# The weight stream's linears read both halves of x as one operand of 512 columns, and ScalarE makes the high half of the weights

## The chip, the core and the metric

The kernel is one program on one core of one Trainium2 chip. The metric is the time of one execution on the device, in microseconds; the median of three runs is the number that counts. The engines are TensorE (PE in the profile, with PEld for its weight loads), VectorE (DVE), ScalarE (ACT), GpSimd (POOL) and SyncE (SP, which here issues the loads of weights).

## What is computed

A two-layer block of 256 tokens with 1024 features (two SwiGLU networks, a mixer of convolution, HGRN2 and RWKV7, and cross-attention over 256 memory rows), and after it a second two-layer block (attention and a mixture of 64 experts). The change touches the plain matrix products of the first block and one of the second:

```python
def swiglu_ffn(x, w_in, w_out):
    gate, up = jnp.split(x @ w_in, 2, axis=-1)
    return (jax.nn.silu(gate) * up) @ w_out

for l in range(DEPTH):                                              # DEPTH = 2
    h = h + FFN_RES * swiglu_ffn(rmsnorm(h, ffn1_norm[l]), ffn1_w_in[l], ffn1_w_out[l])
    p = rmsnorm(h, mix_norm[l]) @ w_mix_in[l]
    ...
    h = h + y @ w_mix_out[l]
    h = h + memory_cross_attention(rmsnorm(h, xattn_norm[l]), rmsnorm(mem, mem_norm[l]),
                                   xattn_wq[l], xattn_wkv[l], xattn_wo[l])
    h = h + FFN_RES * swiglu_ffn(rmsnorm(h, ffn2_norm[l]), ffn2_w_in[l], ffn2_w_out[l])
```

The results are float32. w_in is 1024 x 5632, w_out 2816 x 1024, w_mix_in 1024 x 3712.

## The kernel before

**Split products.** TensorE gets its operands in the type float32r, which keeps fewer bits. A float32 number is therefore split in two: its rounded "high" half, and the rest ("low"). A product a·b is computed as ah·bh + ah·bl + al·bh. `mm3` (L370) issues these three matmuls for one block of weights: the 128 x 128 block is the stationary operand (its high half twice, its low half once) and the moving operand is one half of x^T, 128 features by 256 tokens. All three add up in the same 256 columns of a PSUM bank.

**The stream.** `Stream` (from L109) feeds the weights in the order in which they are used. A chunk is 32 blocks (128 x 4096 numbers, 2 MB). SyncE loads chunk c into one of three slots when TensorE has finished chunk c-3. `split(c)` makes the halves: one operation casts the raw weights into one of two high slots (L130), the second subtracts and writes the low half over the raw weights (L131). When TensorE's program comes to the first block of chunk c, `blocks` marks chunk c-1 as released and records `split(c+1)` at this place. The cast of c+1 waits until its data has arrived and until TensorE has finished chunk c-1, since that chunk held the high slot. `cancel(c)` turns the split of a chunk that is used unsplit into small idle operations; `prepare` records a split ahead of its place.

**Queues.** Each engine's work is a list in program order (`Queue`, L33). Operations of VectorE and ScalarE also wait for the one before them. So a waiting operation holds all that stands behind it on its engine, and the order of recording is the order of execution.

**The linears.** `linear` (L425) computes nm tiles of 128 output features; each takes one of eight PSUM banks and sums over kt blocks, and `evac` then takes the result out of the bank. `ffn` has its own loop for w_in: for each of FT = 22 tiles i it computes gate and up (eight blocks each) in the two halves of one bank, multiplies both by the inverse RMS in one operation of 512 columns, applies SiLU to the gate on ScalarE (`silu[i]`), and `product(i-1)` multiplies gate and up and splits the result (the cast on VectorE, the subtraction on GpSimd). w_in is 352 blocks, 11 chunks; w_out is 176 blocks, eight tiles of 22. In w_out, w_mix_out (64 blocks) and xattn_wo (64) the evacuation adds to the residual X, and `Normed.add` makes both halves of the next stage's input and a Square on ScalarE. Ahead of w_mix_out, `memory_squares` lets ScalarE square eight tiles of the memory, which wait for their load. Ahead of the first linear stand eight scalings and eight squares of x on ScalarE.

The linears of 256 tokens are, for each of the two layers, 2 x 528 blocks of the two feed-forward networks, 232 of w_mix_in, 64 each of w_mix_out, xattn_wq, the K half of xattn_wkv and xattn_wo; with na_w_out (64) that is 3152 blocks, 98.5 chunks. The V half of xattn_wkv and the second block's other products use the stream as well but other forms of matmul; the experts have their own buffers and their own splitting.

## Time and profile before

| | before |
|---|---|
| median of 3 runs | 3906.31 us |
| runs | 3905.23 to 3908.49 us |
| the profiled execution's own time | 3905.64 us |
| its span, first to last instruction | 3903.5 us |
| TensorE busy | 3486.5 us (89%) |
| VectorE busy | 2813.5 us (72%) |
| ScalarE busy | 1163.5 us (30%) |
| mean granted TensorE clock | 0.94 |

A share of busy time is a mean over stages: the first block of the computation lasts until about 1770 us, the experts fill 2105 to 2790 and 3190 to 3840 us. What a change is worth is read in the stage in which it acts, from the wait that ends last there. TensorE's granted clock is given as a share of 2.4 GHz.

### The profile page before, as it was taken

The numbers are of one execution on the slowest core, as the hardware profiler recorded it, in microseconds if no ns is written. First come the engines' busy times: TensorE is split into PE (matmuls) and PEld (weight loads), VectorE is DVE, ScalarE is ACT, GpSimd is POOL, SyncE is SP. The second block draws the span as 40 slices with busy tenths as digits, with TensorE's granted clock in tenths as the row PEclk, the third lists the DMA queues.
The fourth block names the chain that finished last, engine by engine and source line by source line (L and its number), as shares of the span: only waits on it lengthen the run. The fifth ranks groups of instructions, "written<-read, shape, count | busy, mean of one in ns | idle before, by whom it ended". The sixth has DMA issues, their size and how long they took to land. (4 is left out here: it accounts for less than half of the span.)

```text
span 3903.5 us, 51678 instructions
## 1 busy us (share of the span) xinstructions
PE 3486.5 (89%) x20728; PEld 2837.5 (73%) x20728; DVE 2813.5 (72%) x3240; ACT 1163.5 (30%) x1539; POOL 439.6 (11%) x459
## 2 busy tenths in 40 slices
PE   8996878999996879997888999999559889999995
PEld 8993778999993778996555776677348656776774
DVE  8866687888876677887757777777274677777774
ACT  1003101101003101101322565565210245655562
POOL 0000200000000200100001121122001111221220
PEclk9997889999996889998999999999779989999998
DMA  6547023454556023551015999999433159999993
GB/s 238 185 183 280 1 86 124 172 191 175 192 196 256 1 78 128 184 195 65 22 53 195 363 368 363 359 359 372 180 137 119 54 191 336 338 346 335 337 340 127
DMA packets 118927, 802.65 MB, mean 206 GB/s; under 512 B 33808, under 2 KB 34832, under 8 KB 48272
## 3 DMA queue, kind: packets, MB, share of 16 engines
q1 hardware_dynamic: 77040, 714.17, 49.6%
q0 software_dynamic: 40592, 83.99, 6.0%
q8 instruction: 166, 2.72, 0.3%
q10 hardware_dynamic: 1040, 1.05, 0.1%
q14 instruction: 89, 0.73, 0.1%
HBM read 812.18 MB, written 71.83 MB: 226 GB/s over the span
## 5 line engine op out<-in xcount | busy, mean ns | idle before, releaser
L368 PE MATMUL ps<-arena_r,ring_r 128*128 128x256 f32 (+1 forms) x10224 | 1305.1, 289 | 84.2 <-DVE arena L400 24.7
L368 PEld LDWEIGHTS ps<-arena_r,ring_r 128*128 128x128 f32 x10224 | 1265.3, 190 | 120.9 <-DVE arena L400 25.8
L1875 PE MATMUL ps<-ring_r,arena_r 128*128 128x512 f32 x1880 | 555.1, 398 | 7.0 <-DVE arena_r L1891 7.0
L416 ACT ACTIVATE arena<-arena 128x256 f32<-128x256 f32 (+3 forms) x298 | 144.4, 485 | 1292.0 <-DVE arena L400 782.8
L131 DVE TENSOR_TENSOR ring_r<-ring,ring_r 128x4096 fp32r<-128x4096 f32 (+2 forms) x117 | 509.7, 4356 | 4.0
L1875 PE MATMUL ps<-ring,arena 128*128 128x512 f32 x1032 | 464.1, 592 | 1.6 <-DVE arena L1927 1.6
L1872 DVE TENSOR_TENSOR ring_r<-ring,arena_hi 128x2048 fp32r<-128x2048 f32 x152 | 348.5, 2293 | 97.0 <-ACT arena_hi L1871 89.1
L1875 PEld LDWEIGHTS ps<-ring_r,arena_r 128*128 128x128 f32 x1880 | 351.9, 189 | 82.3 <-DVE arena_r L1891 7.9
L1875 PE MATMUL ps<-arena_hi,arena_r 128*128 128x512 f32 x1216 | 400.8, 397 | 0.0
L368 PE MATMUL ps<-arena 128*128 128x128 f32 (+5 forms) x1728 | 262.7, 338 | 105.1 <-DMA arena<-yd_dram 40.5
L130 DVE CAST ring_r<-ring 128x4096 fp32r<-128x4096 f32 (+2 forms) x117 | 291.9, 2495 | 71.3 <-PE ps L368 59.0
L1875 PEld LDWEIGHTS ps<-ring,arena 128*128 128x128 f32 x1032 | 195.4, 190 | 198.0 <-issue 185.2
L368 PEld LDWEIGHTS ps<-arena 128*128 128x128 f32 (+1 forms) x1728 | 205.7, 216 | 155.8 <-ACT arena L420 52.1
L1872 DVE TENSOR_TENSOR ring_r<-ring,ring_r 128x2048 fp32r<-128x2048 f32 x106 | 243.0, 2292 | 74.8 <-ACT ring_r L1871 69.0
L1871 ACT CAST arena_hi<-ring 128x2048 fp32r<-128x2048 f32 x152 | 290.0, 1908 | 13.7 <-ACT arena_r L1890 0.7
L1875 PEld LDWEIGHTS ps<-arena_hi,arena_r 128*128 128x128 f32 x1216 | 229.1, 188 | 48.7
L1891 DVE TENSOR_TENSOR arena_r<-ps,arena_r 128x512 fp32r<-128x512 f32 x258 | 178.4, 692 | 97.6 <-ACT arena_r L1890 83.7
L1956 POOL DMA_INDIRECT yd_dram<-arena,small x129 | 129.8, 1006 | 1015.1 <-ACT arena_r L1890 930.3
L1871 ACT CAST ring_r<-ring 128x2048 fp32r<-128x2048 f32 x106 | 202.6, 1912 | 36.8 <-PE ps L368 19.7
L400 POOL TENSOR_TENSOR arena_r<-arena,arena_r 128x256 fp32r<-128x256 f32 (+1 forms) x104 | 84.2, 810 | 978.5 <-DVE arena_r L388 978.5
L1941 ACT COPY arena<-ps 128x512 f32<-128x512 f32 x129 | 75.5, 585 | 397.2 <-PE ps L1875 397.2
L421 DVE COPY arena<-ps 128x128 f32<-128x128 f32 (+3 forms) x172 | 68.8, 400 | 152.2 <-PE ps L368 139.3
(192 smaller groups left out, 3333.4 us busy)
## 6 DMA issues: line engine op xcount, KB each, us to landing
ring<-wexp_dram SPq DMA_DIRECT2D x387, 1024.0 KB, 8.3
ring<-stream_dram SPq DMA_DIRECT2D x145, 2048.0 KB, 7.7
arena<-yd_dram POOLq DMA_DIRECT2D x12, 2048.0 KB, 10.2
xd_dram<-arena POOLq DMA_DIRECT2D x6, 512.0 KB, 9.9
consts_sb<-consts_dram SPq DMA_DIRECT2D x1, 2241.5 KB, 15.8
arena<-xd_dram,small POOLq DMA_INDIRECT x129, 10.3
yd_dram<-arena,small POOLq DMA_INDIRECT x129, 8.2
arena<-mem_dram POOLq DMA_DIRECT2D x2, 1024.0 KB, 5.3
```

The lines of the kernel that those rows point to most:

```text
L130: self.dve(lambda e, h=h, r=r: e.tensor_copy(h, r), self.arrived(c), self.released.get(c - NHI), after)
L131: toks.append(self.dve(lambda e, h=h, r=r, w=w: e.tensor_tensor(w, r, h.bitcast(F32), ALU.subtract)))
L368: return PE(lambda e: e.matmul(ps, lhsT=lhsT, rhs=rhs, start=start, stop=stop, skip_group_check=True), *after, inc=inc)
L400: return q(lambda e: e.tensor_tensor(out_, a, b, op), *after, **kw)
L416: return ACTQ(lambda e: e.activation(out_, a, f, bias=bias, scale=scale), *after, **kw)
L421: return q(lambda e: e.tensor_copy(out_, a), *after, **kw)
L1871: t = Ac(lambda e: e.copy(hi, src), got(n), free)
L1872: split_tok[n] = Dv(lambda e: e.tensor_tensor(lo, src, hi.bitcast(F32), ALU.subtract), t)
L1875: return P(lambda e: e.matmul(out_, lhsT=x, rhs=y, start=st_, stop=sp_, skip_group_check=True), *after, inc=inc)
L1891: t2 = Dv(lambda e, hi=hi, lo=lo, ps=ps: e.tensor_tensor(lo, ps[:, :], hi.bitcast(F32), ALU.subtract), t2)
L1941: fn = (lambda e, dst=dst, ps=ps: e.copy(dst, ps[0:S, :])) if nn else \
L1956: Po.raw(lambda e: e.indirect_dma_start(out=yd, out_offset=bass.IndirectOffsetOnAxis(ap=pair_of[0:S, b0 + i:b0 + i + 1], axis=0), in_=YB[i ...
```

## The change

`mm3` is replaced in the 256-token linears by `mm2`: one matmul of the weights' high half with 512 columns, the low and the high half of x side by side (an access pattern of two pieces, `pair`), and one of the weights' low half with the 256 columns of x's high half. The first writes all 512 columns of a bank, the second adds to the upper 256. The two halves of the bank are then added: ScalarE copies the lower one to a temporary, VectorE adds the upper one. In w_in, gate and up take a bank each, and the multiplication by the inverse RMS then works on SBUF. In `split`, the cast moves from VectorE to ScalarE; the subtraction stays and waits for it. This holds for all chunks of the stream. `cancel` and its idle operations follow. In xattn the high halves of its output are put in another region.

```diff
@@ Stream.split
-            self.dve(lambda e, h=h, r=r: e.tensor_copy(h, r), self.arrived(c), self.released.get(c - NHI), after)
-            toks.append(self.dve(lambda e, h=h, r=r, w=w: e.tensor_tensor(w, r, h.bitcast(F32), ALU.subtract)))
-        self.ahead[c] = (toks, len(self.dve.ops))
+            t = self.act(lambda e, h=h, r=r: e.copy(h, r), self.arrived(c), self.released.get(c - NHI), after)
+            ops.append((self.act, self.act.ops[-1]))
+            toks.append(self.dve(lambda e, h=h, r=r, w=w: e.tensor_tensor(w, r, h.bitcast(F32), ALU.subtract), t))
+            ops.append((self.dve, self.dve.ops[-1]))
+        self.ahead[c] = (toks, ops)
...
+        def mm2(ps, a, b, start, stop, *after, inc=False):
+
+            (ah, al), (bh, both) = a, b
+            mm(v3(ps[:, :], 256), ah, both, start, False, after)
+            return mm(ps[:, 256:512], al, bh, False, stop, inc=inc)
...
+            def pair(self, k):
+
+                hi, lo = self.hi(k), self.lo(k)
+                n = hi.offset - lo.offset
+                d = max(0, lo.offset + 2 * n - NA)
+                both = arena_r[:, lo.offset - d:lo.offset - d + 2 * n].rearrange("p (o w) -> p o w", o=2)
+                return as_r(hi)[:, 0:256], both[:, :, d:d + 256]
@@ linear
+                if wide:
+                    c = tmp.v(256 * (m % 4), 256)
+                    t = act(c, ps[:, 0:256], ACT.Copy, t, summed.get(m - 4))
+                    t = summed[m] = tt(DVE, ps[:, 0:256], ps[:, 256:512], c, ALU.add, t)
                 tok = evac(m, ps, t)
@@ ffn
             for i in range(FT):
-                ps, w = B.take()
+                s = S.v(512 * (i % 4), 512)
                 for half, c0 in ((0, 0), (1, 2816)):
+                    ps, w = B.take()
                     for k in range(KT):
                         wb, a = W.blocks(w_in, 128 * k, c0 + 128 * i)
-                        t = mm3(ps[:, 256 * half:256 * half + 256], wb, uh.at(k), k == 0, k == KT - 1, w, a, uh.tok[k],
-                                inc=k == KT - 1)
-                if i == 0:
-                    pre.finish()
-                s = S.v(512 * (i % 4), 512)
-                t = tt(DVE, v3(s, 256), v3(ps[:, :], 256), rs2, ALU.mult, t, pre.rs_tok)
-                B.leave(ps, t)
+                        t = mm2(ps, wb, uh.pair(k), k == 0, k == KT - 1, w, a, uh.tok[k], inc=k == KT - 1)
+                    if i == 0 and half == 0:
+                        pre.finish()
+                    h = s[:, 256 * half:256 * half + 256]
+                    t = act(h, ps[:, 0:256], ACT.Copy, t, hh.tok.get(i - 4))
+                    t = tt(DVE, h, ps[:, 256:512], h, ALU.add, t)
+                    B.leave(ps, t)
+                t = tt(DVE, v3(s, 256), v3(s, 256), rs2, ALU.mult, pre.rs_tok)
                 silu[i] = act(s[:, 0:256], s[:, 0:256], ACT.Silu, t)
                 if i:
                     product(i - 1)
```

How the order on the engines changes is seen in two places. The first is VectorE in the middle of a feed-forward network's w_in, one chunk. Before (L400 on `ps` is the multiplication by the inverse RMS, L400 on `arena` the product of gate and up, L388 the cast of its split, L130 and L131 the weights' split):

```order
L400 TENSOR_TENSOR arena<-ps,mrow 128x512
L400 TENSOR_TENSOR arena<-arena 128x256
L388 CAST arena_r<-arena 128x256
L400 TENSOR_TENSOR arena<-ps,mrow 128x512
L400 TENSOR_TENSOR arena<-arena 128x256
L388 CAST arena_r<-arena 128x256
L130 CAST ring_r<-ring 128x4096
L131 TENSOR_TENSOR ring_r<-ring,ring_r 128x4096
```

VectorE at the same place now (L415 is the old L400, L395 the old L388, L132 the old L131):

```order
L415 TENSOR_TENSOR arena<-ps,arena 128x256 x2
L415 TENSOR_TENSOR arena<-arena,mrow 128x512
L415 TENSOR_TENSOR arena<-arena 128x256
L395 CAST arena_r<-arena 128x256
L415 TENSOR_TENSOR arena<-ps,arena 128x256 x2
L415 TENSOR_TENSOR arena<-arena,mrow 128x512
L415 TENSOR_TENSOR arena<-arena 128x256
L395 CAST arena_r<-arena 128x256
L132 TENSOR_TENSOR ring_r<-ring,ring_r 128x4096
```

Four additions have come in and the cast of the weights has gone. ScalarE at that place now, with what each row waits for (L431 on `ps` is the copy of a bank's lower half, L431 on `arena` the SiLU, L130 the cast of the weights; before, only the SiLUs stood here):

```order
L130 CAST ring_r<-ring 128x4096 [waits s_act,s_w2]
L431 ACTIVATE arena<-ps 128x256 [waits s_act,s_pool,s_pe]
L431 ACTIVATE arena<-ps 128x256 [waits s_act,s_pe]
L431 ACTIVATE arena<-arena 128x256 [waits s_act,s_dve]
L431 ACTIVATE arena<-ps 128x256 [waits s_act,s_pool,s_pe]
L431 ACTIVATE arena<-ps 128x256 [waits s_act,s_pe]
L431 ACTIVATE arena<-arena 128x256 [waits s_act,s_dve]
L130 CAST ring_r<-ring 128x4096 [waits s_act,s_w0]
```

The cast stands right behind a SiLU, which waits for VectorE. The second place is ScalarE at w_mix_out of layer 0. Before (the row of x16 is the eight squares of the memory and the eight squares of the residual, then come the square roots of two norms):

```order
L416 ACTIVATE small<-small 128x12
L416 ACTIVATE arena<-arena 128x256 x16
L416 ACTIVATE mrow<-mrow 128x256 x2
L420 COPY arena<-ps 128x256 x4
```

ScalarE at the same place now (the first cast is that of w_mix_out's first chunk, the x8 row the squares of the memory, then the cast of its second chunk, and for each tile a copy of a bank and a square of the residual):

```order
L431 ACTIVATE small<-small 128x12
L130 CAST ring_r<-ring 128x4096
L431 ACTIVATE arena<-arena 128x256 x8
L130 CAST ring_r<-ring 128x4096
L431 ACTIVATE arena<-ps 128x256
L431 ACTIVATE arena<-arena 128x256
L431 ACTIVATE arena<-ps 128x256
L431 ACTIVATE arena<-arena 128x256
L431 ACTIVATE arena<-ps 128x256
L431 ACTIVATE arena<-arena 128x256
L431 ACTIVATE arena<-ps 128x256
L431 ACTIVATE arena<-arena 128x256
```

The casts that stood on VectorE between its own operations now stand between ScalarE's squares.

## Rows read from the trace of the kernel before

**Rows 1.** the page's section 1: busy us, share of the span, instructions

```profile
PE 3486.5 (89%) x20728; PEld 2837.5 (73%) x20728; DVE 2813.5 (72%) x3240; ACT 1163.5 (30%) x1539; POOL 439.6 (11%) x459
```

**Rows 2.** busy us (x instructions) of each engine, granted clock, two stretches

```profile
100.00:150.00 50.00, 50.00 (x427) 50.00 (x426) 44.50 (x38) 3.77 (x9) 7.86 (x11) 1.00 0.54 192
1500.00:1550.00 50.00, 44.64 (x239) 36.40 (x237) 32.60 (x66) 9.15 (x26) 0.00 (x0) 1.00 0.31 109
```

**Rows 3.** timeline, one chunk of w_in: start us, us, engine, line, what

```profile
101.98 2.86 DVE L130 CAST ring_r<-ring 128x4096 fp32r<-128x4096 f32 x1
104.88 4.43 DVE L131 TENSOR_TENSOR ring_r<-ring,ring_r 128x4096 fp32r<-128x4096 f32 x1
109.41 0.69 DVE L400 TENSOR_TENSOR arena<-ps,mrow 128x512 f32<-128x512 f32 x1
110.14 0.42 ACT L416 ACTIVATE arena<-arena 128x256 f32<-128x256 f32 x1 [8.66 <-DVE arena L400]
110.21 0.42 DVE L400 TENSOR_TENSOR arena<-arena 128x256 f32<-128x256 f32 x1
110.67 0.29 DVE L388 CAST arena_r<-arena 128x256 fp32r<-128x256 f32 x1
111.04 0.74 POOL L400 TENSOR_TENSOR arena_r<-arena,arena_r 128x256 fp32r<-128x256 f32 x1 [8.35 <-DVE arena_r L388]
...
113.29 2.86 DVE L130 CAST ring_r<-ring 128x4096 fp32r<-128x4096 f32 x1
```

**Rows 4.** timeline of w_mix_in: VectorE's casts of two successive chunks

```profile
251.79 2.30 DVE L130 CAST ring_r<-ring 128x4096 fp32r<-128x4096 f32 x1
...
263.09 2.29 DVE L130 CAST ring_r<-ring 128x4096 fp32r<-128x4096 f32 x1
```

**Rows 5.** timeline of na_w_in's K half: ScalarE's copies of every second bank

```profile
2958.41 0.59 ACT L420 COPY arena<-ps 128x512 f32<-128x512 f32 x1 [10.63 <-PE ps L368]
...
2969.39 0.59 ACT L420 COPY arena<-ps 128x512 f32<-128x512 f32 x1 [10.40 <-PE ps L368]
```

**Rows 6.** groups by line and shape: count, busy us, mean ns of one

```profile
L1871 ACT CAST arena_hi<-ring 128x2048 fp32r<-128x2048 f32 x152 | 290.0, 1908 | 13.7 <-ACT arena_r L1890 0.7
...
L416 ACT ACTIVATE arena<-arena 128x256 f32<-128x256 f32 x205 | 85.8, 418 | 863.9 <-DVE arena L400 582.7 <-DVE arena L408 234.8 <-DMA arena<-mem_dram 38.4
...
L416 ACT ACTIVATE arena<-arena 128x512 f32<-128x512 f32 x42 | 26.5, 630 | 171.9 <-DVE arena L400 103.8 <-DVE arena L443 66.3
...
L420 ACT COPY arena<-ps 128x256 f32<-128x256 f32 x49 | 18.2, 372 | 144.0 <-PE ps L368 131.6 <-PE ps L397 10.4
...
L400 DVE TENSOR_TENSOR arena<-ps,arena 128x256 f32<-128x256 f32 x38 | 16.1, 425 | 8.5 <-PE ps L368 5.0 <-DVE arena_r L408 0.5
```

**Rows 7.** timeline of the start of the program

```profile
12.04 3.56 ACT L416 ACTIVATE arena<-arena 128x256 f32<-128x256 f32 x8
12.96 0.70 DVE L130 CAST ring_r<-ring 128x1024 fp32r<-128x1024 f32 x1
13.70 1.23 DVE L131 TENSOR_TENSOR ring_r<-ring,ring_r 128x1024 fp32r<-128x1024 f32 x1
...
14.98 8.37 PE L368 MATMUL ps<-arena_r,ring_r 128*128 128x256 f32 x48 [14.98 <-DVE ring_r L131]
```

**Rows 8.** timeline of w_mix_out and the start of xattn_wq, layer 0

```profile
539.87 2.29 DVE L130 CAST ring_r<-ring 128x4096 fp32r<-128x4096 f32 x1
...
543.02 3.57 ACT L416 ACTIVATE arena<-arena 128x256 f32<-128x256 f32 x8 [19.05 <-DMA arena<-mem_dram]
546.73 0.42 DVE L400 TENSOR_TENSOR arena<-ps,arena 128x256 f32<-128x256 f32 x1
...
548.16 0.42 DVE L400 TENSOR_TENSOR arena<-ps,arena 128x256 f32<-128x256 f32 x1
...
567.80 4.42 DVE L131 TENSOR_TENSOR ring_r<-ring,ring_r 128x4096 fp32r<-128x4096 f32 x1
...
596.84 3.36 PE L368 MATMUL ps<-arena_r,ring_r 128*128 128x256 f32 x16 [2.61 <-DVE ring_r L131]
```

More of the change, by code:

```diff
@@ L318, in build @@
                    ring_r[:, NSLOT * CH * 128:(NSLOT + NHI) * CH * 128],
-                   [es.enter_context(nc.semaphore(f"s_w{i}")) for i in range(NSLOT)], PE, DVE,
-                   lambda e: e.memset(scrap[:, 3:4], 0.0))
+                   [es.enter_context(nc.semaphore(f"s_w{i}")) for i in range(NSLOT)], PE, DVE, ACTQ,
+                   {DVE: lambda e: e.memset(scrap[:, 3:4], 0.0), ACTQ: lambda e: e.copy(scrap[:, 2:3], con("col"))})
         A_par = Arrival(es.enter_context(nc.semaphore("s_par")))
@@ L423, in build, with linear @@
         B = Banks(psb)
-        def linear(key, r0, c0, nm, xs, evac, *after, kt=KT, n=256, between=None):
+        def linear(key, r0, c0, nm, xs, evac, *after, kt=KT, n=256, between=None, tmp=None):
             toks = []
+            wide, summed = tmp is not None, {}
             for m in range(nm):
@@ L545, in evac @@
                 return t
-            return linear(w_out, 0, 0, KT, hh, evac, kt=FT)
+            return linear(w_out, 0, 0, KT, hh, evac, kt=FT, tmp=S)
         MB, MF = psb[6:8], psb[5]
@@ L624, in evac @@
                 return pre.scale(P(m), ps[:, 0:256], t)
-            pt = linear(("w_mix_in", l), 0, 0, 29, uh, evac, between=pre.finish)
+            pt = linear(("w_mix_in", l), 0, 0, 29, uh, evac, between=pre.finish, tmp=Yr)
             W.mode(True)
@@ L699, in evac2 @@
                 return t
-            linear(("w_mix_out", l), 0, 0, KT, yh, evac2, f)
+            linear(("w_mix_out", l), 0, 0, KT, yh, evac2, f, tmp=Reg(wk, 1024))
             return mem
@@ L1277, in xattn @@
             tq = linear(("xattn_wq", l), 0, 0, KT, uh, lambda m, ps, t: pre.scale(Qr.v(256 * m, 256), ps[:, 0:256], t),
-                        between=norms)
-            tk = linear(("xattn_wkv", l), 0, 0, KT, mh, to(Kr))
+                        between=norms, tmp=Or)
+            tk = linear(("xattn_wkv", l), 0, 0, KT, mh, to(Kr), tmp=MV)
             W.align(4)
```

22 lines of the change are left out of this document (12 added, 10 removed).

## The prediction, made before the changed kernel was run

> **What bounds the kernel now.** I read the page's busy times first: TensorE is busy 89% of the span, VectorE 72%, ScalarE 30% [rows 1]. These are means, so next the busy time by stretch. In w_in (100 to 150 us) TensorE is busy for all of 50.00 us, VectorE for 44.50, ScalarE for 3.77 [rows 2]. So TensorE sets the pace there and VectorE is close behind. The timeline shows why it holds: the weights' cast starts every 11.31 us (101.98 to 113.29), and cast plus subtraction end 7.33 us after the cast's start [rows 3], four microseconds before TensorE needs the chunk. In w_mix_in the distance of two casts is 11.30 us [rows 4]. That is a chunk of 96 matmuls of 256 columns, 117.7 ns each, 353.1 ns for a block.
>
> **TensorE's part.** The new block is one matmul of 512 columns and one of 256. What 512 columns cost is shown where such matmuls run densely: from one of ScalarE's copies to the next but one, 48 matmuls, 10.98 us pass [rows 5], 228.8 ns each. The new block is 228.8 + 117.7 = 346.5 ns, 6.6 ns less, a chunk 11.09 instead of 11.30 us. The number of columns is the same; only one start of a matmul is saved. Over 3152 blocks (98.5 chunks) that is -20.8 us if TensorE set the pace in all of them. No row shows a moving operand of two pieces. If it costs nothing extra the term stands; I take 0, with up to 4 ns (the block then saves under half) as the upper bound.
>
> The Trainium skill ("TensorE: Matmul & The Clock Gate", section "Wait — 56ns, not 53.3ns?") gives N / 2.4 + 2.5 ns from start to start, thus 109.2 and 215.8 ns, and a saving of 2.5 ns a block, 7.9 us in all. The trace disagrees, both sizes are slower here, and I go by the rows.
>
> **The weights' split.** VectorE loses the cast (2.29 to 2.86 us [rows 3, 4]), ScalarE gets it. ScalarE's cast of 2048 columns takes 1.908 us; 256 and 512 columns take 0.418 and 0.630 us, so 0.205 + 0.83 per thousand columns, and 4096 columns 3.61 us [rows 6]. The subtraction remains 4.43 us [rows 3]. Cast and subtraction are still in series, 8.1 instead of 7.3 us, and now the first stands in one queue and the second in the other. Each queue is held by what its head waits for.
>
> **w_in, the largest term.** The rows of the order show a circle. At the start of chunk c the cast of c+1 stands on ScalarE behind the SiLU of the last tile; this SiLU waits for VectorE's multiplication; that stands behind all evacuations of chunk c-1, and these stand behind the subtraction of chunk c. So from the end of one subtraction to the end of the next there pass, on VectorE and ScalarE one after the other, with 0.04 us from one operation to the next (110.10 to 110.14) and 0.10 after the subtraction (109.31 to 109.41) [rows 3]:
> - 0.10 wait, then four additions of 0.425 [rows 6] + 0.04: 1.86;
> - two multiplications of 512 columns, 0.69 + 0.04 [rows 3]: 1.46;
> - one product 0.42 + 0.04 and one cast 0.29 + 0.04 [rows 3]: 0.79 (the second pair runs beside ScalarE's cast);
> - about 0.11 in which the third addition waits for ScalarE's copy (0.372 us [rows 6], behind the first SiLU);
> - SiLU 0.42 + 0.04, the weights' cast 3.61 + 0.04, the subtraction 4.43.
> The sum is 12.86 us. TensorE's chunk is 11.09. So VectorE and ScalarE, neither of them full, set 12.86 us a chunk and TensorE waits 1.77 us at each start of a chunk. This takes hold once the slack of the start is used up: measured from TensorE's end of chunk c-1 the way copy, addition, multiplication, SiLU, cast, subtraction is 10.2 us, 0.9 less than a chunk. So chunks 1 and 2 are on time, chunk 3 is 0.9 late, and chunks 4 to 12 are 1.77 late each (12 is the first split of w_out made behind the last SiLU). That is 0.9 + 9 x 1.77 = 16.8 us for each of four networks, 67 us. In w_out the way is shorter: after a subtraction one evacuation's addition and residual, a Square, cast and subtraction, about 9.6 us, under 11.09, and TensorE leads again. In the second layer's first network w_in begins in the middle of a chunk; there the last hidden tiles come behind a subtraction and w_out waits some 2 us for them. Together +69 us.
>
> The cover named: were the cast not behind the SiLU, it would start at the release of the high slot and end in time, and the 67 us would be nothing.
>
> **w_mix_out and xattn_wq.** ScalarE's cast of w_mix_out's second chunk stands behind the eight squares of the memory, which wait for its load and run from 543.02 to 546.59 [rows 8]. The cast ends at 550.3 and the subtraction at 554.9; before, both ended at 546.6 [rows 8]. TensorE has been done with the first chunk since about 551.4, so it waits 3.5 us. Then the four evacuations come, 1.43 us each before (546.73 to 548.16 [rows 8]), 1.43 + 0.47 = 1.9 now, and the next cast stands behind the Square of the fourth: 554.9 + 7.2 gives 562.1, cast to 565.8, subtraction to 570.3. The same once more for tiles 4 to 7: evacuated at 578.0, cast to 581.2, subtraction to 585.7, where it ended at 572.22 before [rows 8]: 13.5 us later. The norms and the memory's halves behind it stay as long, four evacuations of xattn_wq get 0.47 longer, and the next subtraction does not contain the cast (-2.3): TensorE's wait for it, which ended at 596.84 [rows 8], ends 13 us later. For both layers: +26 us.
>
> **Small terms.** (a) Start: the first cast now stands behind the eight squares (12.04 to 15.60); 1024 columns take 1.05 us and the subtraction 1.23, so TensorE starts at about 18.0 instead of 14.98 [rows 7]: +3. (b) At the end of a w_out inside a chunk the last evacuation stands behind a subtraction that ends 8.2 instead of 6.8 us after the chunk's start, and has an addition more: 1.9 us, three times; at xattn_wo four evacuations of +0.47 and the cast behind a Square: +2.3, twice; na_w_out's end +0.9. Together +11. (c) In the second block's first attention the cast comes into ScalarE's row of copies, squares and roots: 0 to 7, taken as +3; VectorE loses casts there, which may give 3 back. (d) The second chunk of w_mix_in and the others with four evacuations of two operations a chunk: copy 0.4, cast 3.65, subtraction 4.43, done 8.6 us after the start, hidden. GpSimd, SyncE's loads (2 us a chunk ahead at least) and the experts are not moved.
>
> **Sum.** -20.8 + 69 + 26 + 3 + 11 + 3 = +91 us; the 58 chunks in which TensorE does not lead are already counted by their waits over 11.09. The profiled execution took 3905.64 us, the median is 0.67 us above it; I add the sum to the median: about 3998 us.
>
> **Rivals.**
> 1. *The busy times decide.* In w_in VectorE's work for a chunk falls from 10.1 us to 4.43 + 1.70 + 1.38 + 1.42 = 8.9. If waits in the queues were covered by this slack everywhere, only the -20.8 and the start's +3 would be left: about 3888 us, faster than before. It decides if the cast gets ahead of SiLU and squares. The order speaks against it, as does every row in which an engine's operations lie one behind the other. Chance 0.05. By the Trainium skill (the same page, "Engine queue depths") ScalarE and VectorE are strictly in order; by that rule this rival is out.
> 2. *The circle of w_in does not close*, because a link of it is shorter than I think (the circle must come under 11.1 us, 1.8 less), but the waits at w_mix_out and the small terms are there: 3998 - 69, about 3930 us. Chance 0.10. Half of the circle's excess would give 3965, in my range.
> 3. *The two-piece operand costs 4 ns.* This counts only in the 54 chunks outside w_in, since w_in does not go by TensorE: 54 x 32 x 4 ns = 7 us, 4005 us. Chance 0.08, and hardly to be told from the forecast.
> 4. *TensorE's clock falls in the new waits.* A chunk with 1.8 us of waiting in 12.9 is 86% busy. In a stretch with 44.64 of 50 us busy the granted clock was 1.00 [rows 2], which speaks against. If the clock went to 1.2 GHz in a tenth of the 98 chunks, each would be up to 11 us longer beyond its wait: some 60 to 100 us more, 4080 us. Chance 0.07.
> The forecast itself, with its waits, gets 0.70.
>
> **The numbers.** The circle is uncertain by 0.5 us (hand-overs of 0 to 0.08 us over eleven steps), times 38 chunks 19 us; the pair's price up to 7; w_mix_out 8; the rest 8. The forecast's own range is 3965 to 4030. The range of 8 in 10 must take part of rival 2: 3945 to 4035. What a measurement of this kernel can tell from no change is 0.2%, 8 us. Faster by more: 0.05 (rival 1); within: 0.02; slower by more: 0.93.
>
> **What would show it.** In the profile after, in w_in: the weights' casts on ScalarE every 12.9 us, of 3.6 us each, right behind a SiLU; VectorE idle before each subtraction with ScalarE's cast as the releaser; TensorE idle some 1.8 us once a chunk before a matmul that waits for L132, with 64 matmuls and 11.1 us between. In w_mix_in no such wait and a chunk of 11.1 us. At w_mix_out waits of about 3.5 and 4 us for L132. TensorE's first matmul at 18 us. I am wrong if the casts in w_in come every 11.1 us, or if a chunk of w_mix_in is not shorter than 11.30 us.

## The result, and the profile after

The changed kernel takes 4024.65 us, median of 4 runs (4019.54 to 4033.64), against 3905.77 us (3903.91 to 3908.49) for the kernel before on the same chip: a ratio of 1.0305, 95% interval 1.0286 to 1.0324. It is 119 us slower; the forecast was 3998, in a range of 3945 to 4035. The profiled execution's span grew from 3903.5 to 4022.8 us.

The page of the kernel after, first its busy times (us, share of the span, instructions), then three of its groups (busy us, mean ns of one | idle time just before them and what ended most of it):

```profile
PE 3521.6 (88%) x17576; PEld 2705.4 (67%) x17576; DVE 2666.5 (66%) x3457; ACT 1711.2 (43%) x1998; POOL 430.4 (11%) x459
...
L369 PE MATMUL ps<-arena_r,ring_r 128*128 128x512 f32 (+1 forms) x7072 | 1323.0, 348 | 170.7 <-DVE ring_r L132 96.1
...
L132 DVE TENSOR_TENSOR ring_r<-ring,ring_r 128x4096 fp32r<-128x4096 f32 (+2 forms) x117 | 510.8, 4366 | 389.3 <-ACT ring_r L130 388.2
...
L130 ACT CAST ring_r<-ring 128x4096 fp32r<-128x4096 f32 (+2 forms) x117 | 417.1, 3565 | 89.4 <-PE ps L369 74.8
```

TensorE has 3152 matmuls fewer than in [rows 1] and is busy 35 us longer. VectorE is busy 147 us less. TensorE has waited 96 us for VectorE's subtraction (L132), and that subtraction 388 us for ScalarE's cast: VectorE, which was relieved, stands idle in front of it. The means of [rows 1] would not have told this.

The stretch of w_in that [rows 2] shows, now:

```profile
100.00:150.00 50.00, 45.39 (x254) 38.85 (x254) 33.60 (x44) 24.02 (x28) 5.92 (x8) 1.00 0.44 164
```

TensorE 45.39 us of 50 where it was busy for all 50, at the same granted clock of 1.00. The timeline of one chunk there, which answers to [rows 3]:

```profile
99.83 0.95 DVE L415 TENSOR_TENSOR arena<-ps,arena 128x256 f32<-128x256 f32 x2
99.87 11.54 PE L369 MATMUL ps<-arena_r,ring_r 128*128 128x512 f32 x64 [1.67 <-DVE ring_r L132]
100.82 0.69 DVE L415 TENSOR_TENSOR arena<-arena,mrow 128x512 f32<-128x512 f32 x1
101.54 0.42 ACT L431 ACTIVATE arena<-arena 128x256 f32<-128x256 f32 x1 [5.30 <-DVE arena L415]
...
102.08 0.86 ACT L431 ACTIVATE arena<-ps 128x256 f32<-128x256 f32 x2
...
102.49 0.95 DVE L415 TENSOR_TENSOR arena<-ps,arena 128x256 f32<-128x256 f32 x2 [0.20 <-ACT arena L431]
103.48 0.69 DVE L415 TENSOR_TENSOR arena<-arena,mrow 128x512 f32<-128x512 f32 x1
104.21 0.42 ACT L431 ACTIVATE arena<-arena 128x256 f32<-128x256 f32 x1 [1.27 <-DVE arena L415]
...
104.72 3.62 ACT L130 CAST ring_r<-ring 128x4096 fp32r<-128x4096 f32 x1
...
108.37 4.43 DVE L132 TENSOR_TENSOR ring_r<-ring,ring_r 128x4096 fp32r<-128x4096 f32 x1 [3.40 <-ACT ring_r L130]
...
112.94 1.27 PE L369 MATMUL ps<-arena_r,ring_r 128*128 128x512 f32 x6 [1.53 <-DVE ring_r L132]
```

From one start of TensorE to the next 13.07 us pass (99.87 to 112.94), where [rows 3] has 11.31. The circle is readable in it: the cast at 104.72 stands behind the SiLU at 104.21 on ScalarE; that waited for VectorE's multiplication at 103.48; that stands behind four additions, and these stood behind the subtraction before. Cast, subtraction, evacuations, SiLU, one at a time on two engines, and TensorE, the third, waits at its end.

ScalarE's copies of every tile's first 256 columns in w_mix_in, in place of [rows 4]. The four tiles of a chunk lie between the first and the last row:

```profile
249.48 0.38 ACT L431 ACTIVATE arena<-ps 128x256 f32<-128x256 f32 x1 [2.44 <-PE ps L369]
...
260.79 0.38 ACT L431 ACTIVATE arena<-ps 128x256 f32<-128x256 f32 x1 [2.44 <-PE ps L369]
```

11.31 us for 32 blocks, 353.4 ns a block, as before. The start, which answers to [rows 7], and w_mix_out, which answers to [rows 8] (its times are later by the 22.5 us lost so far):

```profile
15.89 4.05 ACT L130 CAST ring_r<-ring 128x1024 fp32r<-128x1024 f32 x3
...
18.25 3.35 PE L369 MATMUL ps<-arena_r,ring_r 128*128 128x512 f32 x9 [18.25 <-DVE ring_r L132]
```

```profile
565.56 3.57 ACT L431 ACTIVATE arena<-arena 128x256 f32<-128x256 f32 x8 [15.62 <-DMA arena<-mem_dram]
569.21 3.62 ACT L130 CAST ring_r<-ring 128x4096 fp32r<-128x4096 f32 x1
572.86 4.42 DVE L132 TENSOR_TENSOR ring_r<-ring,ring_r 128x4096 fp32r<-128x4096 f32 x1 [10.53 <-ACT ring_r L130]
...
577.34 12.99 PE L369 MATMUL ps<-arena_r,ring_r 128*128 128x512 f32 x64 [3.76 <-DVE ring_r L132]
```

The cast stands behind the memory's squares, the subtraction ends at 577.28, TensorE starts at 577.34. VectorE's reciprocals, of which every norm has one, serve as marks from here on: each stands in the profile of every kernel, so their times tell how far a kernel is behind the kernel before at that place. The reciprocal in the norms behind w_mix_out comes 13.5 us later, against the one ahead of it (22.2 behind before, then 35.7); in layer 1 it is 13.1.

A short stretch there, in the form of [rows 2]:

```profile
598.00:606.00 8.00, 6.55 (x17) 4.99 (x18) 4.53 (x6) 4.37 (x3) 0.00 (x0) 0.57 0.00 0
```

The granted clock is 0.57, so TensorE ran for most of it at the lower of its two levels, 1.2 GHz; at the same place of the kernel before (565 to 573 us) it was 1.00. The 32 matmuls that sum up the norms' squares took 9.22 us here and 7.07 before. This is hardly on the path: VectorE reads the first norm's sum only behind its subtraction, in both kernels (607.93 here, 572.22 before).

### The profile page after: what moved, and what is told of

Same layout as the page of the kernel before. It is cut to its first block and busy times, and to the rows that moved or that the text cites. A ratio compares the mean times of both kernels' runs of the same rounds, so it can differ in the third digit from the quotient of the medians.

```text
span 4022.8 us, 46543 instructions
## 1 busy us (share of the span) xinstructions
PE 3521.6 (88%) x17576; PEld 2705.4 (67%) x17576; DVE 2666.5 (66%) x3457; ACT 1711.2 (43%) x1998; POOL 430.4 (11%) x459
## 3 DMA queue, kind: packets, MB, share of 16 engines
q10 hardware_dynamic: 1040, 1.05, 0.1%
## 5 line engine op out<-in xcount | busy, mean ns | idle before, releaser
L369 PE MATMUL ps<-arena_r,ring_r 128*128 128x512 f32 (+1 forms) x7072 | 1323.0, 348 | 170.7 <-DVE ring_r L132 96.1
L369 PEld LDWEIGHTS ps<-arena_r,ring_r 128*128 128x128 f32 x7072 | 1120.1, 192 | 368.2 <-DVE ring_r L132 104.3
L132 DVE TENSOR_TENSOR ring_r<-ring,ring_r 128x4096 fp32r<-128x4096 f32 (+2 forms) x117 | 510.8, 4366 | 389.3 <-ACT ring_r L130 388.2
L431 ACT ACTIVATE arena<-arena 128x256 f32<-128x256 f32 (+3 forms) x298 | 144.3, 484 | 744.1 <-DVE arena L415 547.8
L130 ACT CAST ring_r<-ring 128x4096 fp32r<-128x4096 f32 (+2 forms) x117 | 417.1, 3565 | 89.4 <-PE ps L369 74.8
L1896 ACT CAST arena_hi<-ring 128x2048 fp32r<-128x2048 f32 x152 | 290.0, 1908 | 13.5 <-ACT ring_r L1896 0.4
L431 ACT ACTIVATE arena<-ps 128x256 f32<-128x256 f32 (+1 forms) x350 | 135.1, 386 | 242.3 <-PE ps L369 212.3
L415 POOL TENSOR_TENSOR arena_r<-arena,arena_r 128x256 fp32r<-128x256 f32 (+1 forms) x104 | 84.3, 811 | 1084.2 <-DVE arena_r L395 1084.2
## 6 DMA issues: line engine op xcount, KB each, us to landing
arena<-yd_dram POOLq DMA_DIRECT2D x12, 2048.0 KB, 10.9
arena<-xd_dram,small POOLq DMA_INDIRECT x129, 10.3
```

What stands on the lines that cost most here:

```text
L130: t = self.act(lambda e, h=h, r=r: e.copy(h, r), self.arrived(c), self.released.get(c - NHI), after)
L132: toks.append(self.dve(lambda e, h=h, r=r, w=w: e.tensor_tensor(w, r, h.bitcast(F32), ALU.subtract), t))
L369: return PE(lambda e: e.matmul(ps, lhsT=lhsT, rhs=rhs, start=start, stop=stop, skip_group_check=True), *after, inc=inc)
L415: return q(lambda e: e.tensor_tensor(out_, a, b, op), *after, **kw)
L431: return ACTQ(lambda e: e.activation(out_, a, f, bias=bias, scale=scale), *after, **kw)
L1896: t = Ac(lambda e: e.copy(hi, src), got(n), free)
```

## The experiments

Each kernel is timed beside the kernel before on its chip. That one's medians there were 3909.29 (first four), 3910.16 (next four), 3905.45 (e11, e12) and 3908.79 us (e15, e16), so kernels of different groups are compared by their ratios.

### One part alone: e1 and e2

e1 takes the cast back to VectorE and keeps the wide products:

```diff
-            t = self.act(lambda e, h=h, r=r: e.copy(h, r), self.arrived(c), self.released.get(c - NHI), after)
+            t = self.dve(lambda e, h=h, r=r: e.tensor_copy(h, r), self.arrived(c), self.released.get(c - NHI), after)
```

> The changed kernel with one part undone: the weights' cast is back on VectorE, the products stay in the new form (512 + 256 columns, the added copies and additions). Theory of the circle (queues in series set the pace in w_in): VectorE alone is the circle now, cast 2.87 + 0.04, subtraction 4.43 + 0.10, four additions 1.98, two multiplications 1.46, two products and casts 1.58 = 12.5 us a chunk against TensorE's 11.31, so some 1.1 us of waiting in about 40 chunks, +45; the long waits at w_mix_out are gone, only longer evacuations remain, +10 to +15. About 3965 us. Rival, the cast on ScalarE is the whole of the loss: 3906 us, no waits in w_in.

Measured: 3998.35 us (3996.24 to 4009.38), ratio 1.0236 [1.0206, 1.0266]. Timeline of a chunk of w_in in e1:

```profile
102.07 2.84 DVE L130 CAST ring_r<-ring 128x4096 fp32r<-128x4096 f32 x1
...
104.94 4.42 DVE L132 TENSOR_TENSOR ring_r<-ring,ring_r 128x4096 fp32r<-128x4096 f32 x1
...
109.47 0.95 DVE L415 TENSOR_TENSOR arena<-ps,arena 128x256 f32<-128x256 f32 x2
109.52 11.41 PE L369 MATMUL ps<-arena_r,ring_r 128*128 128x512 f32 x64 [1.13 <-DVE ring_r L132]
...
114.74 2.83 DVE L130 CAST ring_r<-ring 128x4096 fp32r<-128x4096 f32 x1
```

A cast every 12.67 us. Here VectorE is one row without a gap of note (about 18.5 of every 20 us busy): the four additions that the wide products need do not fit beside cast and subtraction. So the wide products alone are 92 us too long (by the ratio), without any ScalarE cast.

e2 does the reverse, the old three products everywhere (with w_in's old evacuation) and the cast on ScalarE:

```diff
-            wide, summed = tmp is not None, {}
+            wide, summed = False, {}
...
-                        t = mm2(ps, wb, uh.pair(k), k == 0, k == KT - 1, w, a, uh.tok[k], inc=k == KT - 1)
+                        t = mm3(ps[:, 256 * half:256 * half + 256], wb, uh.at(k), k == 0, k == KT - 1, w, a, uh.tok[k],
+                                inc=k == KT - 1)
```

> The other part undone: three matmuls of 256 columns as before, without copies and additions, but the weights' cast on ScalarE. Theory of the circle: in w_in it is subtraction 4.53, multiplication 0.73, product and cast 0.79, multiplication 0.73, SiLU 0.50, cast 3.66 = 10.9 us, under TensorE's 11.31, so no waits there; the casts behind the squares remain: start +3.3, w_mix_out and xattn_wq about +7 a layer, tails and the second block +5 to +10. About 3935 us. Rival, the additions on VectorE are the whole of the loss (its load): 3906 us. Rival, the cast on ScalarE costs its 0.8 us a chunk wherever it stands: 98 x 0.8 = +78, 3984 us.

Measured: 3924.14 us (3914.12 to 3931.65), ratio 1.0035 [1.0021, 1.0048], 14 us over the kernel before. Timeline of w_in in e2:

```profile
104.57 3.64 ACT L130 CAST ring_r<-ring 128x4096 fp32r<-128x4096 f32 x1
...
108.24 4.43 DVE L132 TENSOR_TENSOR ring_r<-ring,ring_r 128x4096 fp32r<-128x4096 f32 x1 [3.38 <-ACT ring_r L130]
112.77 0.69 DVE L415 TENSOR_TENSOR arena<-ps,mrow 128x512 f32<-128x512 f32 x1
...
115.88 3.64 ACT L130 CAST ring_r<-ring 128x4096 fp32r<-128x4096 f32 x1
```

Every 11.31 us, TensorE's own time: without the additions the circle closes. Its loss lies mostly at w_mix_out, where the norm's reciprocal slips by 10.3 us in layer 0 (from 5.9 behind the kernel before to 16.2) and 9.6 in layer 1 (12.9 to 22.5). About half of it comes back by the norm behind the cross-attention (10.9 and 18.3 behind). Both parts together cost 119, alone 92 and 14. Neither median met its expectation: e2's lies 11 us under it, e1's 33 us over. In e1 the four feed-forward networks lost 20.0, 14.5, 17.4 and 18.6 us by the reciprocals, some 70 together where 45 had been put; VectorE's own row of 12.67 us instead of 12.5 explains some 7 of the 25 between, the rest was not traced.

### The cast ahead of the evacuation: e3 and e4

e3 lets ScalarE's cast and VectorE's subtraction be recorded ahead of the evacuation of the tile that ends a chunk:

```diff
+    def close(self):
+        c = len(self.specs) // CH
+        if len(self.specs) % CH == 0 and c and not self.plain and c - 1 not in self.released:
+            self.released[c - 1] = self.pe.mark()
...
+            self.split(c + 1)
```

> The changed kernel in which only the place of a chunk's split in the queues is moved: when a linear's or w_in's tile ends a chunk, the split of the chunk after next is recorded before this tile's evacuation, so the cast does not stand behind copy, multiplication and SiLU (or Square) of that tile. Same operations, same counts. Theory of the circle: w_in falls from 13.07 to TensorE's 11.31 us a chunk, -70 us, and w_mix_out and xattn_wq lose one or two waits for Squares, -10 to -16: about 3940 us. Rival, load (VectorE and ScalarE are slowed by their number of operations, not by the order): unchanged, 4020 us.

Measured: 4083.97 us (4077.36 to 4086.4), ratio 1.044 [1.0412, 1.0468]. A miss of 144 us, and in the wrong direction from the kernel after. The timeline of e3 at the end of w_in, and the window's row (busy us by engine, then the granted clock):

```profile
167.73 0.39 ACT L441 ACTIVATE arena<-ps 128x256 f32<-128x256 f32 x1
...
168.22 3.62 ACT L130 CAST ring_r<-ring 128x4096 fp32r<-128x4096 f32 x1
...
171.87 4.43 DVE L132 TENSOR_TENSOR ring_r<-ring,ring_r 128x4096 fp32r<-128x4096 f32 x1 [3.30 <-ACT ring_r L130]
176.40 0.42 DVE L425 TENSOR_TENSOR arena<-ps,arena 128x256 f32<-128x256 f32 x1
...
178.42 0.72 POOL L425 TENSOR_TENSOR arena_r<-arena,arena_r 128x256 fp32r<-128x256 f32 x1 [9.65 <-DVE arena_r L405]
...
179.19 1.01 PE L379 MATMUL ps<-arena_r,ring_r 128*128 128x512 f32 x2 [8.55 <-POOL arena_r L425]
```

```profile
160.00:180.00 20.00, 9.96 (x53) 7.99 (x51) 15.29 (x18) 6.42 (x8) 2.38 (x4) 0.87 0.29 106
```

The circle only turned: in w_in a cast still comes every 13.07 us (102.85, 115.92, 128.99), because what stands ahead of it on ScalarE now (the copy at 167.73) stands itself behind the SiLU of the tile before, and that behind VectorE. One link was put behind the split in place of ahead of it, and a circle's length does not depend on where one starts to count. New is the price at its end: the last evacuation of w_in stands behind cast and subtraction, w_out's first tile waits 8.55 us at its 21st block for the hidden tiles that are still missing, and in this stretch the granted clock fell to 0.87, with TensorE busy 9.96 of 20 us. From 175 to 185 us it was 0.50: the first matmuls behind the long wait ran at 1.2 GHz. By the reciprocal behind the first network e3 is 33.6 us behind, 9.9 more than the kernel after, and at w_mix_out's norms in layer 0 it is 19.9 (31.8 to 51.7) in place of 13.5. Time lost in a chunk and time lost at a boundary are two accounts, and I had looked only at the first.

e4 is e3 with the memory's squares recorded after w_mix_out's first tile:

```diff
-            mem = memory_squares(l, f)
+            mem = []
...
+                   between=lambda: mem.extend(memory_squares(l, f)))
```

> As the run before, and the eight squares of the memory are recorded after w_mix_out's first tile, so that the cast of its second chunk does not stand behind them. Theory: the wait of TensorE at w_mix_out's second chunk (3.5 us) is gone in both layers and what it pushed behind it, -7 us or more against the run before: about 3930 us. Rival, this wait is hidden by VectorE's later work in xattn_wq: 0 against the run before.

Measured: 4071.32 us (4069.98 to 4075.61), ratio 1.0415 [1.0387, 1.0442], 12.7 under e3. The total was missed with e3's. What the squares cost at w_mix_out is told by the difference: about 6 us a layer in the medians.

### The circle itself: e8

If cast and subtraction follow one another because each is one instruction for the whole chunk, smaller pieces overlap them: VectorE subtracts the first quarter while ScalarE casts the second. Queues, places and products stay.

```diff
-        for a, b in ((0, 1024), (1024, 2048), (2048, 4096)) if c == 0 else ((0, 4096),):
+        for a, b in ((0, 1024), (1024, 2048), (2048, 4096)) if c == 0 else [(q, q + 1024) for q in range(0, 4096, 1024)]:
```

(Where a chunk is not filled to its end, two waits for VectorE's last subtraction were added, on ScalarE and at the load of the slot.) The edit does a second thing: a block of weights waits for the piece that it lies in, so TensorE may begin a chunk when its first quarter is split and need not wait for all of it.

> The changed kernel, with each chunk split in four pieces of 1024 columns (the high half by ScalarE, the subtraction by VectorE) where one of 4096 stood. Same products, same queues, same engines, four times as many instructions for it. Theory (the circle): in w_in a chunk took 13.07 us because VectorE stood idle for the 3.6 us of the cast, and ScalarE's cast for VectorE's work of the tile ahead. In quarters the subtraction begins after the first quarter of the cast (about 1 us), so that the circle is 1.0 + 4 x 1.15 + 5.0 = 10.6 us, under TensorE's 11.3: TensorE's waits of 1.5 us a chunk go, 77 us over the four networks, and some of the waits at w_mix_out with them (up to 20). 3940, and 3925 to 3950. Rival: the waits come from VectorE's own load (more instructions, more time): 4024 to 4045. Rival: TensorE's 512 columns in two pieces cost more in w_in than elsewhere: no less than 3990.

Measured: 3929.21 us (3923.53 to 3935.23), ratio 1.0053 [1.0034, 1.0072]: 95 us under the kernel after. The rival by which VectorE's load makes the waits is refuted: its busy time in w_in rose to 41.91 of 50 us. The window and the timeline of e8:

```profile
100.00:150.00 50.00, 50.00 (x285) 43.53 (x284) 41.91 (x65) 27.58 (x44) 6.67 (x9) 1.00 0.48 172
```

```profile
102.15 0.69 DVE L421 TENSOR_TENSOR arena<-arena,mrow 128x512 f32<-128x512 f32 x1
...
106.04 4.30 ACT L131 CAST ring_r<-ring 128x1024 fp32r<-128x1024 f32 x4
...
107.12 5.22 DVE L133 TENSOR_TENSOR ring_r<-ring,ring_r 128x1024 fp32r<-128x1024 f32 x4 [0.83 <-ACT ring_r L131]
...
112.44 0.95 DVE L421 TENSOR_TENSOR arena<-ps,arena 128x256 f32<-128x256 f32 x2
```

The subtraction starts 1.08 us after the cast, not 3.65, and TensorE is busy for all of the stretch. The cast comes every 11.28 us instead of every 13.07. An earlier start of TensorE within a chunk could not have changed this distance, so it is the circle that got shorter. But the new circle is not 10.6 us: four subtractions take 5.22 and not the 4.6 I had reckoned, the evacuations with both SiLUs 4.9, and 1.08 + 5.22 + 0.10 + 4.9 is 11.3, just TensorE's 11.31. The circle was loosened by the 1.8 us that it needed and no more. This matters below.

### The price of a pair: e5 and e12

In e5 the two halves of a tile of x lie side by side, so that the operand of 512 columns is one contiguous run:

```diff
-            hh = Halves(lambda k: H.v(256 * k, 256), lambda k: HH.v(256 * k, 256))
+            hh = Halves(lambda k: H.v(512 * k, 256), lambda k: H.v(512 * k + 256, 256))
```

> The changed kernel, with the high and the low half of each tile of x laid side by side, so that the operand of 512 columns is one run of the row and not two pieces of 256. Theory: the eight columns-of-256 prices show why a pair cost 353.4 ns as before: the operand of two pieces is no cheaper than two products of 256. In one piece it should cost 228.8 ns, the pair 346.6, a chunk of w_mix_in 11.09 us in place of 11.31. In w_in nothing, since the circle of ScalarE and VectorE (13.07 us a chunk) decides there. Some 1,200 to 2,100 pairs outside w_in save 6.8 ns each, 8 to 14 us: about 4012. Rival: the pieces don't matter and the pair stays at 353.4 ns: 4024, chunk of w_mix_in 11.31.

Measured: 4021.74 us (4017.22 to 4031.55), ratio 1.0294 [1.0273, 1.0316], the ratio of the kernel after within its interval. ScalarE's copies in w_mix_in in e5, four tiles apart:

```profile
259.54 0.39 ACT L433 ACTIVATE arena<-ps 128x256 f32<-128x256 f32 x1 [1.06 <-PE ps L369]
...
270.84 0.39 ACT L433 ACTIVATE arena<-ps 128x256 f32<-128x256 f32 x1 [1.05 <-PE ps L369]
```

11.30 us: one piece or two makes no difference. My theory of the two pieces fell; the rival stood.

e12 is e8 with the same matmuls in another order, first eight of 512 columns, then the eight of 256:

```diff
-            return mm(ps[:, 256:512], al, bh, False, stop, inc=inc)
+            held.append((al, bh))
+            if len(W.specs) % 8 == 0 or stop:
+                for n, (al, bh) in enumerate(held):
+                    end = n == len(held) - 1
+                    t = mm(ps[:, 256:512], al, bh, False, stop and end, inc=inc and end)
+                held.clear()
```

> Wide products with the split in quarters, and eight wide products of 512 columns one behind the other, then the eight of 256. The same matmuls, another order. It asks why a pair takes 353.4 ns here when dense matmuls of 512 columns took 228.8 in na_w_in. Theory A: the alternation costs it (two sizes in turn, or a weight load that doesn't find its cover behind the short one): grouped, the eight take 1.83 us and 0.94, a chunk of w_mix_in 11.09 us, and the whole 15 to 20 us less than with the quarters alone, about 3912. Theory B: 512 columns cost 235.6 ns in this stage, whatever stands beside them: chunk 11.31, 3929, no change to the kernel with quarters.

Measured: 3921.99 us (3916.9 to 3924.09), ratio 1.0039 [1.0025, 1.0054]. In w_mix_in of e12, four tiles apart, and then its casts in w_in:

```profile
256.90 0.39 ACT L445 ACTIVATE arena<-ps 128x256 f32<-128x256 f32 x1 [0.23 <-PE ps L375]
...
267.93 0.39 ACT L445 ACTIVATE arena<-ps 128x256 f32<-128x256 f32 x1 [0.23 <-PE ps L375]
```

```profile
105.69 4.31 ACT L131 CAST ring_r<-ring 128x1024 fp32r<-128x1024 f32 x4
...
116.98 4.31 ACT L131 CAST ring_r<-ring 128x1024 fp32r<-128x1024 f32 x4
```

A chunk is 11.03 us, 344.7 ns a pair in place of 353.4: theory A, the alternation costs it, 8.7 ns a pair. Theory B, that 512 columns cost more in this stage whatever stands beside them, is refuted. (344.7 is also 1.8 ns less than 228.8 + 117.7, so prices taken from rows of one size do not add up exactly in either order.) The whole kernel gained little of it (the intervals of its ratio and e8's overlap; against their own befores the medians differ by 2.5 us, the ratios by 0.0014 or 5.5 us), since in w_in the circle still takes 11.29 us (105.69 to 116.98): as soon as TensorE gets faster than 11.29, ScalarE and VectorE lead again. Why the alternation costs is open: that a load of 128 columns of weights does not find enough cover behind the shorter matmul would fit, but no row here tells it from other causes.

### What can be had: e9, e10, e11, e15, e16

e9 is the old three products with the cast on ScalarE in quarters: e2's edit and e8's, on the kernel after.

```diff
-            wide, summed = tmp is not None, {}
+            wide, summed = False, {}
...
-        for a, b in ((0, 1024), (1024, 2048), (2048, 4096)) if c == 0 else ((0, 4096),):
+        for a, b in ((0, 1024), (1024, 2048), (2048, 4096)) if c == 0 else [(q, q + 1024) for q in range(0, 4096, 1024)]:
```

> The old three products of 256 columns, the cast on ScalarE, and the split in quarters. With whole chunks this was 3924, 18 us over the kernel before, of which some 20 lay in front of w_mix_out's norms. Theory: what is left of the cast's price is the latency of cast plus subtraction (8.1 us before the first block may be used, 2.2 us in quarters) where the queues have been held up: 3908, and 3900 to 3915. Rival: it is the memory's squares ahead of the cast on ScalarE, which quarters don't move: 3920 to 3925.

Measured: 3904.16 us (3897.61 to 3908.7), ratio 0.9989 [0.998, 0.9999]. As forecast, quarters return what e2 had lost.

e10 has all three repairs with the wide products: the edits of e5, e8 and e4 (squares).

> Wide products on one contiguous operand, the split in quarters, and the squares of the memory recorded after w_mix_out's first tile. Theory: the three repairs add up: 3940 for quarters, 12 less for the squares (as the pair of kernels that differed in them alone showed), and 6.8 ns on each of some 3,000 pairs, 20 us, since TensorE decides in w_in too: 3908, and 3895 to 3925. Rival: quarters leave TensorE waiting in w_in, so that the pairs give nothing there: 3930 or more.

Measured: 3917.07 us (3911.02 to 3923.23), ratio 1.0021 [1.001, 1.0032]. 12 us under e8. It differs from e8 in the squares and in e5's edit; since e5 alone changed nothing, the 12 us are put down to the squares. The 20 us from the pair are absent, as e5 explains. Even repaired, the wide products don't reach the kernel before.

e11 is e9 with the squares later, by e4's edit:

```diff
-            mem = memory_squares(l, f)
+            mem = []
...
+                   between=lambda: mem.extend(memory_squares(l, f)))
```

> The old three products, the cast on ScalarE in quarters, and the squares of the memory recorded after w_mix_out's first tile. With the quarters alone the split on two engines stood at 3904, six us under the kernel before. Theory: of the waits at w_mix_out that are left, the squares cause a few us a layer: 3898, and 3893 to 3904. Rival: in quarters the squares are hidden, since the first quarter is split before them: 3904, no change.

Measured: 3887.38 us (3885.44 to 3891.43), ratio 0.9954 [0.9939, 0.9969], 18 us faster than the kernel before, and 11 better than I expected. TensorE's waits in e11 from 570 to 705 us (us in total, times, longest), and then those from 575 to 705 us in the kernel before:

```profile
PE ps L375 <- ACT arena L441: 2.4, 5, 0.7
PE ps L375 <- DVE arena_r L421: 2.0, 4, 1.5
PE ps L375 <- DVE arena L442: 1.0, 1, 1.0
```

```profile
PE ps L368 <- DVE arena_r L400: 2.7, 8, 1.5
PE ps L368 <- DVE ring_r L131: 2.6, 1, 2.6
PE ps L368 <- DVE arena_r L408: 2.5, 3, 0.8
PE ps L368 <- ACT arena L420: 2.3, 4, 0.7
...
```

The waits at the cross-attention's linears for the weights' low half (2.6) and for x's halves (2.5) are gone. From the reciprocal at 523.5 to the one at 705.5 us of the kernel before, e11 gains 10.7 us, and from 1404.4 to 1585.5 another 10.6: there VectorE has the evacuations and halves of several norms to make, and no longer the weights' cast beside them. The part behind w_mix_out's norms can be compared with e2, which has the cast on ScalarE but neither quarters nor the squares moved: from the norms at 572.8 to the reciprocal at 705.5, e2 gains 5.3 us on the kernel before (16.2 to 10.9 behind), e11 7.8. In layer 1 it is 4.2 (22.5 to 18.3 behind) and 6.3. That speaks for the cast's move as the source of most of this part.

e16 is the kernel before with the squares later and nothing else:

```diff
-            linear(("w_mix_out", l), 0, 0, KT, yh, evac2, f)
+            linear(("w_mix_out", l), 0, 0, KT, yh, evac2, f, between=lambda: mem.extend(memory_squares(l, f)))
```

> The kernel before (cast on VectorE, three products, whole chunks), with one edit: the squares of the memory are recorded after w_mix_out's first tile. It asks whether the 18 us that the squares and the quarters gained over the kernel before need ScalarE's cast at all. Theory A: in the kernel before the cast doesn't stand behind the squares, so moving them gives nothing: 3905, 3900 to 3910, and the gain is owed to VectorE's relief. Theory B: the squares alone delay w_mix_out's evacuations: 3890 to 3896.

Measured: 3909.61 us (3902.19 to 3917.94), ratio 0.9999 [0.9988, 1.0011]. Theory A: the squares hurt only where a cast stands behind them on ScalarE. So the 18 us are not the squares' alone; they need the cast on ScalarE, the quarters or both. How they divide between the two is not shown: the kernel before with its cast on VectorE in quarters was not run. Only e2's gain behind the norms speaks for the relief of VectorE.

e15 is e11 with wide products, grouped as in e12, in the four w_out alone (of the linears only they have kt over KT):

```diff
-            wide, summed = False, {}
+            wide, summed = tmp is not None and kt > KT, {}
```

> The old three products, the split in quarters on ScalarE and the squares later (3887), and only the four w_out with the wide products, grouped by size, where a tile has 22 blocks and its evacuation comes once in 7.6 us. Theory: there TensorE sets the pace, a block costs 344.7 ns grouped in place of 353.4, 5.5 chunks x 0.27 us in each of four networks: 6 us less, 3881. Rival: VectorE's and ScalarE's added operation at each evacuation delays the end of a w_out and the norm behind it by as much: 3887 or a little more.

Measured: 3887.36 us (3879.02 to 3895.16), ratio 0.9941 [0.9923, 0.9959]. The intervals of e11 and e15 overlap, the medians are the same; it can't be told from e11. In its profile 5 us were ahead of e11 by 1585 us and lost again by the end.

## Why the prediction was right, and where it was not

**The sign and the mechanism** were right. The circle was named in the prediction: SiLU, cast, subtraction, four additions. It was put at 12.86 us and is 13.07: a pair of additions takes 0.99 us with its hand-over and not 0.93, the way from the SiLU's start to the cast's 0.51 and not 0.46, and ScalarE's copy holds the third addition a little longer. The forecast of TensorE's wait, 1.77 us a chunk, came out at 1.53 to 1.67 in the rows, and 1.76 by the distance of chunks (13.07 less 11.31). That it fits so closely is luck: both terms of the difference had been put 0.2 us too small. e8 shows that the circle was the cause: it left every operation on its engine and in its queue and shortened the way through cast and subtraction, the casts came every 11.28 us, and the waits for L132 in w_in went from 17.2 us in the first network to none.

**The step that failed is TensorE's part**, the -20.8 us. The pair was put at 228.8 + 117.7 = 346.5 ns and cost 353.4: the gain was nothing. The 228.8 ns came from a stage in which matmuls of 512 columns follow one another [rows 5]; here each stands between two of 256. e12 shows that this is the difference: in groups the same pair costs 344.7. I had named what no row showed (an operand of two pieces, up to 4 ns), and that was not it (e5). The prediction had said "I am wrong if a chunk of w_mix_in is not shorter than 11.30 us"; it is 11.31. Put this term at 0, and the waits over TensorE's chunk shrink too, to 12.86 less 11.31 in 38 chunks, 8 us less: the sum is +104 and the time some 4010 us. The circle's 0.21 us more in 38 chunks brings the 8 us back, and 4018 is 7 us under the measured time. (The sum's remark on 58 chunks in which TensorE does not lead has no working; the waits of w_in stand on 38.)

The Trainium skill ("TensorE: Matmul & The Clock Gate", section "Wait — 56ns, not 53.3ns?") gives a fixed 2.5 ns a matmul beside its columns, by which the pair would save 2.5 ns in any order. The runs here show 0 in alternation and 8.4 grouped, so what a matmul costs here depends on what stands beside it.

**w_in and w_out**, by the reciprocals of the norms, lost 20, 17, 25 and 21 us in the four networks, 84 together (the first without the 3.3 us of the late start). The prediction had 69 us of waits and 6 of the tails there, less 0.21 us on each of 66 chunks, 14, together 61. Of the 23 us between, 6 are the failed step (28 chunks in which TensorE leads) and 8 the circle's 0.21 us in 38 chunks; the other 9 were not traced. Between the networks 4 us were won back, in the mixers.

**w_mix_out** was right: 13 us a layer predicted, 13.5 and 13.1 measured at its norms and 13.7 and 14.2 by the norm behind the cross-attention, with a first wait of 3.76 where 3.5 stood. The second, at xattn_wq, was 2.43 and not 4. Of its cause one half was tried, the squares ahead of the cast: with them moved, the kernels lost 12 us less (e3 to e4, e8 to e10). The other half, the longer evacuations and the next cast behind the fourth Square, is read from the order and the rows only.

**The start**: TensorE's first matmul at 18.25, predicted 18.0. **The second block** lost 7.5 us from 1893 us on (111.9 to 119.4 behind), where some 4 were put. In e5, whose second block is the same program, the profiled execution lost nothing there (116.8 behind, then 114.0), so neither the 7.5 nor the 4 is shown to belong to the change.

**The rivals.** "Busy times decide" is out: VectorE had 147 us less to do and the kernel lost 119. It may be half true where the queues are mended (e11 is 18 us faster than the kernel before, with the same relief and the quarters). "The circle does not close" is out for both parts together, but true for the cast alone (e2). "The two-piece operand costs 4 ns" is out: a pair did cost 7 ns more than forecast, but for another reason (e5, e12). "The clock falls": the granted clock stayed at 1.00 in w_in of the kernel after, with its waits of at most 1.9 us a chunk, so the rival is out where it was priced. It did fall at w_mix_out (0.57 from 598 to 606 us, behind several waits of 1.1 to 2.4 us), and in e3 behind the wait of 8.55 us: waits did bring the clock down there, but not in w_in.

**What I missed** and only the experiments told: most of the loss belongs to the wide products alone (e1: +92), not to the meeting of both parts. Four additions of 0.43 us a chunk on an engine that was busy 44.5 of 50 us [rows 2] have no room beside the cast: 11.31 us of TensorE against 12.67 us of VectorE. With the cast on ScalarE they have room, once the two engines overlap: in e8 VectorE is busy 41.91 of 50 us and TensorE all 50. So the wide products need the cast's move, and the quarters besides.

## What to carry to other kernels

When two in-order engines hand work to each other, add up the way round, operation by operation, and compare it with the period of the engine that shall lead; the busy shares (66% and 43% here) don't show it. Moving one link to another place on the circle doesn't shorten it (e3), cutting a long link in pieces that overlap does (e8). And before an edit saves matmuls by making them larger, take their price from a stage where they stand in the same neighbourhood, and price the second evacuation operation against the engine that makes it.

## What the runs showed of the hardware

- fp32r matmuls with 512 and 256 columns in turn take 353.4 ns a pair, exactly three times 117.8; the same matmuls in groups of eight take 344.7. A moving operand in two pieces of 256 columns costs the same as a contiguous one (11.31 and 11.30 us for 32 pairs).
- ScalarE's cast of 4096 columns takes 3.62 us (VectorE's took 2.3 to 2.9). In quarters it is 1.05 us each, 4.30 with the gaps; VectorE's subtraction of 1024 columns takes 1.24, four of them 5.22 where one of 4096 takes 4.43. So cutting in four costs 0.7 to 0.8 us of each engine a chunk, and saved 1.8 us of the way.
- In e3 the granted clock was 0.87 over 20 us in which TensorE was busy 9.96, and 0.50 (1.2 GHz) from 175 to 185 us, behind a wait of 8.55 us. In the kernel after it stayed at 1.00 in the first network's w_in, with waits of at most 1.7 us and 45.39 of 50 us busy, and was 0.57 from 598 to 606 us, where TensorE had been busy 3.22 of the 8 us before.
